# The next chunk's scores ahead of the gate or modulation unit in TensorE's order of a chunked recurrence

## The chip, the cores and the metric

The kernel runs on one core of a Trainium2 chip. A core has five engines that run their own instruction streams and meet only at semaphores: TensorE (PE, matrix products into PSUM; its weight loads are listed as PEld), VectorE (DVE), ScalarE (ACT), GpSimd (POOL) and SyncE (SP, which here only issues DMAs). The metric is the device time of one launch in microseconds (us).

## What is computed

One inference step of a hybrid decoder layer: two gated linear recurrences side by side (GLA with 4 heads, HGRN2 with 8 heads), gated norms, a merge, a layer norm, a mixture of 64 experts and a second layer norm, for 512 prompt tokens and 8 single decode tokens. The change lies in the prompt's recurrences. Cut to these:

```python
def _gated_linear_recurrence(q, k, v, log_a, s0):
    ...
    def step(s, inp):
        qi, ki, vi, gi = inp
        b = jnp.cumsum(gi, axis=2)
        diff = b[:, :, :, None, :] - b[:, :, None, :, :]
        decay = jnp.exp(jnp.where(mask, diff, -jnp.inf))
        scores = jnp.einsum('bhik,bhjk,bhijk->bhij', qi, ki, decay)
        o = jnp.einsum('bhij,bhjv->bhiv', scores, vi) + jnp.einsum('bhik,bhkv->bhiv', qi * jnp.exp(b), s)
        b_last = b[:, :, -1:, :]
        s_new = s * jnp.exp(b_last[:, :, 0, :, None]) + jnp.einsum('bhjk,bhjv->bhkv', ki * jnp.exp(b_last - b), vi)
        return s_new, o
    ...
```

Each output row is then normed by its root mean square (the root that POOL makes below) and multiplied by a gate of a projection: silu for GLA, sigmoid for HGRN2 (the gate units below).

## The kernel before

All data is float32. The prompt's recurrences are three **groups** of four heads each: group 0 is GLA (256 values per head), groups 1 and 2 are the two halves of HGRN2 (128 values per head). A group has 16 **chunks** of 128 tokens (4 heads x 4 chunks), numbered c = 0 to 15, and chunks go in **pairs** (2k, 2k+1), since the decay factors are made for 256 tokens at a time. Between the groups PE makes the projections of the next one.

Every engine's order is written out by hand, and no scheduler moves anything. An engine takes its instructions strictly in that order.

**PE**, in `recurrence_pe`, loops over c. `update(c)` (L530) is the product that gives the state's increment; it needs `kdT`, the copy that ACT makes (L652) of a transposed factor. `fill` is a piece of other work put into the loop: in group 0 half of a modulation projection (`mod_proj`, L839, 4 products of 512 columns, and in every second chunk `mod_turn`, L848, ahead of it), in groups 1 and 2 one gate projection (`gate_proj`, L865, 8 products of 260 columns). `scores_of(c+1)` makes the next chunk's transposed factor (L511), one block of scores (L513) and 14 blocks of 64x64 (L520); its first wait, on `s_Mq`, is for the pair's factors from DVE. `output(c)` (L537, L540) needs the summed scores of chunk c and ACT's `scale` of chunk c-1 (`s_on`), since both use one PSUM bank. `turn(c-1)` (L548) transposes the output before.

**DVE**, for every c: `mask` (L1631 to L1642, sums the seven levels of scores), `new_state` (L1655 or L1658), in groups 1 and 2 `gate_value` (L595 to L604), then for odd c `diffs` (L1607, eight differences of the pair after the next one) and for even c from 2 to 12 `factored` (L1622 to L1625), which turns the exponentials of pair c/2+1 into the factors that PE's `scores_of(c+2)` waits for. In group 2 DVE takes the turned output too (L1667).

**ACT**, for every c: `square(c-1)` (L659), `take_o` (L677, groups 0 and 1), `gate_tanh` (L588, groups 1 and 2), `scale(c-1)` (L664), then for even c from 2 to 12 `decays(c/2+1)`: Abs (L625) and Exp (L627) over 2048 columns, and after these `copy_kd(c+1)` (L652, L654). In group 0 `copy_rows` (L1230) stands at the head of every second chunk's list. Abs waits for `diffs` of its pair, and stands behind `scale` in ACT's order. **POOL** makes the root of the mean square between `square` and `scale` (L1427, L1429), and applies a gate in group 1 (L612).

The first two pairs' factors of a group are made before its loop (`first_factors`, and DVE's two first `factored`). So six pairs in each group, 2 to 7, have theirs made inside the loop.

Of the kernel before, what the change touches and what calls it, by code (L numbers as in the profile page):

```python
# [128 lines left out]
def decoder_step(nc, xT, small, wgk2, const, route, wq, wexp, st_in, yT, st_prompt, st_out):  # L129
    with ExitStack() as ctx:  # L130
# [306 lines left out]
        def taken(gi, what):  # L437

            return 1 + max(n for n, it in enumerate(ITEMS) if it[:2] == (gi, what))

        def since(eng, s, value):

            if value > 0:
                eng.wait_ge(s, value)
# [33 lines left out]
        FILL = [[("mod", 8 + c) for c in range(16)], [("gate", c) for c in range(16)], [("gate", 16 + c) for c in range(16)]]  # L478
# [23 lines left out]
        def recurrence_pe(pe, gi, fill, last):  # L502
            v, base = GROUPS[gi]["v"], 16 * gi

            def scores_of(n):
                pair, p, c, h, cc = n // 2, n // 2 % 2, n % 2, n // 4 % 4, n % 4
                col_ = slice(c * CH, (c + 1) * CH)
                pe.wait_ge(s_Mq, pair + 1)
                since(pe, s_kdc, n)
                since(pe, s_L0, n)  # L510
                pe.transpose(ps[:, 2, 0:CH], M[:, p, 7, col_], ident)  # L511
                first, second = (slice(c * CH + h2 * HC, c * CH + (h2 + 1) * HC) for h2 in range(2))
                pe.matmul(ps[0:HC, 2, CH:CH + HC], M[:, p, 0, first], M[:, p, 0, second],  # L513
                          start=True, stop=True, tile_position=(0, 0)).then_inc(s_kdt, 1)
                since(pe, s_pm, 3 * n - 5)
                for l in range(1, LEV + 1):
                    for h2, part in enumerate((first, second)):
                        at = slice(cc * CH + h2 * HC, cc * CH + (h2 + 1) * HC)
                        lhs, rhs = (M[:, p, l, part], M[:, p, l, part]) if l < LEV else (k4[:, h, at], q4[:, h, at])
                        mm = pe.matmul(ps[h2 * HC:(h2 + 1) * HC, n % 2, (l - 1) * HC:l * HC], lhs, rhs,  # L520
                                       start=True, stop=True, tile_position=(0, h2 * HC))
                mm.then_inc(s_sc, 1)

            def values(n):
                return V[:, n % 4, n // 4 % 4 * v:(n // 4 % 4 + 1) * v]

            def update(n):
                pe.wait_ge(s_kdc, n + 1)
                since(pe, s_state, n)
                pe.matmul(ps[:, 3, 0:v], kdT[:, n % 2, :], values(n), start=True, stop=True).then_inc(s_u, 1)  # L530

            def output(n):
                o = ps[:, 4, 0:v]
                pe.wait_ge(s_st, n + 1)
                pe.wait_ge(s_L0, n + 1)
                since(pe, s_on, n)
                mm = pe.matmul(o, ST[:, n % 2, :], values(n), start=True, stop=(n % 4 == 0))  # L537
                if n % 4:
                    pe.wait_ge(s_state, n)
                    mm = pe.matmul(o, M[:, n // 2 % 2, 8, n % 2 * CH:(n % 2 + 1) * CH], state[:, n % 4 % 2, 0:v],  # L540
                                   start=False, stop=True)
                mm.then_inc(s_o, 1)

            def turn(n):
                pe.wait_ge(s_on, n + 1)
                since(pe, s_oc, n)
                for j in range(v // P):
                    mm = pe.transpose(ps[:, 6, j * P:(j + 1) * P], on[n % 2][:, j * P:(j + 1) * P], ident)  # L548
                mm.then_inc(s_ot, 1)

            pe.wait_ge(s_zev, taken(gi, "v"))
            pe.wait_ge(s_sz, 1)
            scores_of(base)
            for c in range(17):
                if c < 16:
                    update(base + c)
                    fill(*FILL[gi][c])
                if c + 1 < 16:
                    scores_of(base + c + 1)
                if c < 16:  # L560
                    output(base + c)
                if c:
                    turn(base + c - 1)
            if gi == 0:
                last()
# [259 lines left out]
        def _(pe):  # L825
# [54 lines left out]
            for gi, what, a, b in ITEMS:  # L880
                g = GROUPS[gi]
                if gi and n == taken(gi - 1, "v"):
                    recurrence_pe(pe, gi - 1, fill, lambda: mod_turn(11))
                    pe.wait_ge(s_pm, 48 * gi)
                    pe.wait_ge(s_L0, 16 * gi)
# [32 lines left out]
                mm.then_inc(s_z, 1)  # L918
                n += 1
            recurrence_pe(pe, 2, fill, None)  # L920

            pe.wait_ge(s_zev, len(ITEMS))
# [1257 lines left out]
```

## Time and profile before

| | |
|---|---|
| runs | 1832.88, 1833.12, 1836.98 us; median 1833.12 |
| profiled execution | 1830.96 us, its span 1828.9 us |
| PE busy | 1690.9 us, 92% of the span |
| DVE, ACT, POOL busy | 32%, 25%, 16% of the span |
| granted clock of PE, mean over the span | 0.971 |
| group 0 / 1 / 2 | about 172 to 264 / 356 to 456 / 543.6 to 642.4 us |

Times in the rows are microseconds from the span's start. A row of the timeline is one instruction or a run of equal ones: its start, its length, engine, line, operation, what is written and read, the count, and in brackets the idle time of the engine just before it with what ended that. A long product is listed as two records. Matmuls overlap, so the time that a step takes is read from the start of its first row to the start of the next step's first row. The granted clock is the share of full speed that the chip gave PE: 1.00 is 2.4 GHz, 0.50 is 1.2 GHz.

### The profile page before, as it was taken

The page shows a single profiled execution, that of the slowest core. Times are in us where ns is not written, and L with a number is a line of the kernel's source. Part 1 is how long each engine was busy: PE and PEld are TensorE (multiplying, and loading weights), DVE is VectorE, ACT ScalarE, POOL GpSimd, SP SyncE. Part 2 cuts the span into 40 slices and gives each one's busy share as a digit, 9 for nine tenths or more (in the row PEclk, how much of TensorE's full clock was granted, in tenths as well). Part 3 has the DMA queues.
Part 4 walks back from the last instruction along what each step waited for, and adds up shares of the span by engine and source line. Part 5 has one row for each costly group of instructions (what it writes and reads, how often), then busy time and mean ns, then how long its engine had stood idle before and what let it go on. Part 6 is the DMA issues. An engine that isn't in the chain of part 4 may idle for free.

```text
span 1828.9 us, 26402 instructions
## 1 busy us (share of the span) xinstructions
PE 1690.9 (92%) x8996; PEld 1121.6 (61%) x8996; DVE 579.2 (32%) x1494; ACT 458.1 (25%) x1040; POOL 298.9 (16%) x488
## 2 busy tenths in 40 slices
PE   5999789998999999889998789999999999999985
PEld 2854558577858788678887544554444454444474
DVE  1213750587048733200125811111111111111145
ACT  1314651455134433200002111111111111111223
POOL 0000110023001110000000622222222222222410
PEclk8999999999999999989999789999999999999997
DMA  9213441210120099463111379999999999999361
GB/s 399 81 47 124 170 180 47 93 49 22 76 83 12 4 370 349 155 279 138 57 69 48 138 308 408 418 406 398 403 404 406 402 395 394 382 384 383 148 299 47
DMA packets 57197, 410.31 MB, mean 224 GB/s; under 512 B 12955, under 2 KB 18716, under 8 KB 29986
## 3 DMA queue, kind: packets, MB, share of 16 engines
q1 hardware_dynamic: 36210, 365.65, 50.4%
q0 software_dynamic: 19184, 42.58, 6.1%
q10 hardware_dynamic: 1728, 1.05, 0.2%
q8 instruction: 51, 0.84, 0.2%
q14 instruction: 24, 0.20, 0.0%
HBM read 391.79 MB, written 42.07 MB: 237 GB/s over the span
## 4 chain that ended last, share of the span: by engine, by line
PE 69%; DMA 12%; DVE 9%; ACT 5%; issue 2%; POOL 2%; SPq 0%; POOLq 0%; ACTq 0%; DVEq 0%
PE ps L957 12%; PE ps L1116 11%; PE ps L916 9%; DMA arena<-wexp 9%; PE ps L894 6%; PE ps L1121 5%; PE ps L1140 5%; PE ps L1147 3%; PE ps L997 3%; PE ps L865 2%; DVE arena L1622 2%; ACT arena L625 2%; PE ps L1187 2%; ACT arena L627 2%; PE ps L1102 2%
## 5 line engine op out<-in xcount | busy, mean ns | idle before, releaser
L1116 PE MATMUL ps<-arena 128*128 128x512 f32 x592 | 263.0, 597 | 10.6 <-DMA arena<-wexp 8.9
L1116 PEld LDWEIGHTS ps<-arena 128*128 128x128 f32 x592 | 110.3, 191 | 149.9 <-issue 149.9
L916 PE MATMUL ps<-Hb,arena 128*128 128x260 f32 x768 | 174.0, 391 | 0.0
L916 PEld LDWEIGHTS ps<-Hb,arena 128*128 128x128 f32 x768 | 149.4, 195 | 24.2 <-ACT arena L1260 0.7
L2066 DVE TENSOR_TENSOR arena<-ps,arena 128x256 f32<-128x256 f32 x73 | 26.2, 359 | 413.6 <-ACT arena L1374 413.6
L1485 POOL DMA_INDIRECT yrows<-arena x72 | 74.6, 1036 | 427.4 <-issue 427.4
L957 PE MATMUL ps<-Hb,arena 128*128 128x260 f32 x512 | 125.1, 400 | 14.9 <-DMA arena<-wq 14.4
L1121 PE MATMUL ps<-arena 128*64 128x256 f32 x1152 | 132.3, 382 | 1.7 <-DMA arena<-wexp 0.8
L1140 PE MATMUL ps<-arena 128*128 128x512 f32 x288 | 129.6, 593 | 0.0
L2075 DVE COPY arena<-ps 128x512 f32<-128x512 f32 x108 | 74.6, 691 | 154.5 <-PE ps L1140 108.2
L957 PEld LDWEIGHTS ps<-Hb,arena 128*128 128x128 f32 x512 | 101.6, 200 | 33.1 <-DMA arena<-wq 15.0
L1374 ACT ACTIVATE arena<-ps 128x256 f32<-128x256 f32 x73 | 24.2, 331 | 374.8 <-PE ps L1116 257.6
L865 PE MATMUL ps<-Hb,arena 128*128 128x260 f32 x512 | 117.5, 383 | 0.0
L894 PE MATMUL ps<-arena,Hb 128*128 128x512 f32 x256 | 112.0, 596 | 0.0
L1121 PEld LDWEIGHTS ps<-arena 128*64 128x64 f32 x1152 | 82.6, 137 | 41.5 <-issue 8.0
L865 PEld LDWEIGHTS ps<-Hb,arena 128*128 128x128 f32 x512 | 94.9, 190 | 13.0
L1622 DVE TENSOR_TENSOR arena<-arena 128x256 f32<-128x256 f32 x168 | 60.1, 427 | 101.0 <-ACT arena L627 101.0
L894 PEld LDWEIGHTS ps<-arena,Hb 128*128 128x128 f32 x256 | 48.0, 190 | 64.1 <-issue 60.7
L1140 PEld LDWEIGHTS ps<-arena 128*128 128x128 f32 x288 | 52.0, 190 | 51.6 <-issue 51.6
L1367 ACT ACTIVATE arena<-ps 128x512 f32<-128x512 f32 x111 | 62.4, 595 | 38.7 <-PE ps L1102 37.1
L1758 DVE TENSOR_TENSOR arena<-arena,ps 128x260 f32<-128x260 f32 x32 | 13.6, 424 | 180.7 <-PE ps L957 180.6
L1476 POOL DMA_INDIRECT Hb<-h2rows,arena x58 | 62.5, 1078 | 49.6 <-POOL arena L1474 47.0
(339 smaller groups left out, 2231.8 us busy)
## 6 DMA issues: line engine op xcount, KB each, us to landing
arena<-wexp SPq DMA_DIRECT2D x73, 2048.0 KB, 16.5
arena<-wq SPq DMA_DIRECT2D x44, 2048.0 KB, 7.9
arena<-wexp SPq DMA_DIRECT2D x72, 1024.0 KB, 19.3
arena<-yrows SPq DMA_DIRECT2D x4, 4096.0 KB, 22.5
arena<-st_in SPq DMA_DIRECT2D x8, 1024.0 KB, 10.0
Xb<-vs POOLq DMA_DIRECT2D x16, 512.0 KB, 9.6
st_out<-arena SPq DMA_DIRECT2D x8, 1024.0 KB, 9.9
Xb<-xT SPq DMA_DIRECT2D x2, 2080.0 KB, 17.6
```

Of the source, the lines that this page charges most:

```text
L865: mm = pe.matmul(ps[:, bank, 0:HALF], ring[:, q % 4, m % 4, c, :], H[:, c, lo:lo + HALF], start=(c == 0), stop=(c == KC - 1))
L894: mm = pe.matmul(ps[:, bank, :], H[:, c, b * P:(b + 1) * P], ring[:, q % 4, :, c, :], start=(c == 0), stop=(c == KC - 1))
L916: mm = pe.matmul(ps[:, bank, 0:HALF], ring[:, q % 4, a, c, :], H[:, c, halves[b][0]:halves[b][1]], start=(c == 0), stop=(c == KC - 1))
L957: mm = pe.matmul(ps[:, 5 + k % 3, 0:HALF], ring[:, (Q_P + n) % 4, u, c, :], (H, oa, H, ob)[u][:, c, lo:hi], start=(c == 0), stop=(c == KC ...
L1116: mm = pe.matmul(ps[:, 0, :], xe[:, 0, c, :], GU[k % 4][:, c, :], start=(c == 0), stop=(c == KC - 1))
L1121: mm = pe.matmul(ps[h * SS:(h + 1) * SS, 1, 0:FE], x, GUs[k % 4][:, c, h, :, :], start=(c == 0), stop=(c == KC - 1), tile_position=(0, h * ...
L1140: mm = pe.matmul(ps[:, 4 + hf, :], aT[:, 0, f, :], WD[k % 4][:, f, hf * 512:(hf + 1) * 512], start=(f == 0), stop=(f == 1))
L1367: act.activation(xe[:, k % 2, 4 * hf:4 * hf + 4, :].rearrange("p c n -> p (c n)"), ps[:, 6 + hf, :], ACT.Copy).then_inc(s_xc, 1)
L1476: pool.indirect_dma_start(out=xg[k % 4][:, 0:n], out_offset=None, in_=rows, in_offset=bass.IndirectOffsetOnAxis(ap=idg[:, k % 4:k % 4 + 1] ...
L1485: pool.indirect_dma_start(out=rows, out_offset=bass.IndirectOffsetOnAxis(ap=ida[:, k:k + 1], axis=0), in_=yb[:, k % 2, 0:n], in_offset=Non ...
L1622: dve.tensor_tensor(e, e, kq, ALU.mult)
L2075: dve.tensor_copy(yb[:, k % 2, hf * 512:(hf + 1) * 512], ps[:, 3 if k % 2 else 4 + hf, :]).then_inc(s_yc, 1)
```

## The change

In PE's loop over the chunks the call of `fill` moves from ahead of `scores_of(c+1)` to behind it. Each chunk's list was update, fill, scores of the next chunk, output, turn, and is update, scores of the next chunk, fill, output, turn. Nothing is added or removed, every instruction keeps its waits, and the other four engines' lists are unchanged.

```diff
             for c in range(17):
                 if c < 16:
                     update(base + c)
-                    fill(*FILL[gi][c])
                 if c + 1 < 16:
                     scores_of(base + c + 1)
                 if c < 16:
+                    fill(*FILL[gi][c])
                     output(base + c)
                 if c:
                     turn(base + c - 1)
```

Group 0, PE, a chunk with odd c, before. L530 is the update, L839 the modulation half, L511 to L520 the scores of the next chunk, whose first product waits for the pair's factors (`mq_mk_done`), L537 the output:

```order
L530 MATMUL ps<-arena,Xb 128x256 [waits state_done,kd_copied]
L839 MATMUL ps<-arena,OB 32x512 [waits quad_loaded_3]
L839 MATMUL ps<-arena,OB 32x512 x3
L511 MATMUL ps<-cst,arena 128x128 [waits halves_copied,kd_copied,mq_mk_done]
L513 MATMUL ps<-arena 64x64
L520 MATMUL ps<-arena 64x64 [waits score_sums]
L520 MATMUL ps<-arena 64x64 x13
L537 MATMUL ps<-arena,Xb 128x256 [waits o_scaled,halves_copied,scores_summed]
```

The same chunk now:

```order
L530 MATMUL ps<-arena,Xb 128x256 [waits state_done,kd_copied]
L511 MATMUL ps<-cst,arena 128x128 [waits halves_copied,kd_copied,mq_mk_done]
L513 MATMUL ps<-arena 64x64
L520 MATMUL ps<-arena 64x64 [waits score_sums]
L520 MATMUL ps<-arena 64x64 x13
L839 MATMUL ps<-arena,OB 32x512 [waits quad_loaded_3]
L839 MATMUL ps<-arena,OB 32x512 x3
L537 MATMUL ps<-arena,Xb 128x256 [waits o_scaled,halves_copied,scores_summed]
```

The modulation half stood between the update and the wait for the factors; it now stands between that wait and the output.

Groups 1 and 2, PE, a chunk before, with L865 the gate projection:

```order
L530 MATMUL ps<-arena,Xb 128x128 [waits state_done,kd_copied]
L865 MATMUL ps<-Hb,arena 128x260 [waits gate_value,quad_loaded_3]
L865 MATMUL ps<-Hb,arena 128x260 x7
L511 MATMUL ps<-cst,arena 128x128 [waits halves_copied,kd_copied,mq_mk_done]
L513 MATMUL ps<-arena 64x64
L520 MATMUL ps<-arena 64x64 [waits score_sums]
L520 MATMUL ps<-arena 64x64 x13
L537 MATMUL ps<-arena,Xb 128x128 [waits o_scaled,halves_copied,scores_summed]
```

The same chunk now:

```order
L530 MATMUL ps<-arena,Xb 128x128 [waits state_done,kd_copied]
L511 MATMUL ps<-cst,arena 128x128 [waits halves_copied,kd_copied,mq_mk_done]
L513 MATMUL ps<-arena 64x64
L520 MATMUL ps<-arena 64x64 [waits score_sums]
L520 MATMUL ps<-arena 64x64 x13
L865 MATMUL ps<-Hb,arena 128x260 [waits gate_value,quad_loaded_3]
L865 MATMUL ps<-Hb,arena 128x260 x7
L537 MATMUL ps<-arena,Xb 128x128 [waits o_scaled,halves_copied,scores_summed]
```

Eight products of 260 columns have moved from ahead of the scores to the place just ahead of the output.

## Rows read from the trace of the kernel before

**Rows 1.** PE's waits by who ended them: us in total, times, longest.

```profile
PE ps L530 <- ACT Xb L652: 18.4, 16, 1.5
```

**Rows 2.** PE's timeline, group 0, chunk 9 (a row of chunk 5 at half clock ahead).

```profile
201.31 0.47 PE L511 MATMUL ps<-cst,arena 128*128 128x128 f32 x1 [0.59 <-DVE arena L1625]
...
203.62 1.22 PE L537 MATMUL ps<-arena,Xb 128*128 128x256 f32 x2
...
223.70 0.70 PE L530 MATMUL ps<-arena,Xb 128*128 128x256 f32 x2 [1.49 <-ACT Xb L652]
224.33 1.07 PE L839 MATMUL ps<-arena,OB 128*32 128x512 f32 x8
226.74 0.33 PE L511 MATMUL ps<-cst,arena 128*128 128x128 f32 x1 [1.34 <-DVE arena L1625]
...
228.48 0.70 PE L537 MATMUL ps<-arena,Xb 128*128 128x256 f32 x2 [0.34 <-DVE Xb L1642]
```

**Rows 3.** DVE's timeline, group 0, from one pair's factors to the next pair's.

```profile
223.51 2.50 DVE L1622 TENSOR_TENSOR arena<-arena 128x256 f32<-128x256 f32 x7 [1.82 <-ACT arena L627]
...
226.26 0.42 DVE L1625 TENSOR_TENSOR arena<-arena 128x256 f32<-128x256 f32 x1
...
235.63 2.50 DVE L1622 TENSOR_TENSOR arena<-arena 128x256 f32<-128x256 f32 x7 [1.76 <-ACT arena L627]
```

**Rows 4.** ACT's timeline, group 0: square, scale and Abs after output 9.

```profile
229.64 0.38 ACT L659 ACTIVATE Xb<-ps 128x256 f32<-128x256 f32 x1 [1.24 <-PE ps L540]
...
231.38 0.47 ACT L664 ACTIVATE Xb<-ps,tiny 128x256 f32<-128x256 f32 x1 [0.75 <-POOL tiny L1429]
231.75 1.90 ACT L625 ACTIVATE arena<-arena 128x2048 f32<-128x2048 f32 x1
```

**Rows 5.** PE's timeline, group 1, chunk 5: update, gate projection, scores, output.

```profile
387.17 0.49 PE L530 MATMUL ps<-arena,Xb 128*128 128x128 f32 x2 [1.40 <-ACT Xb L652]
387.49 3.67 PE L865 MATMUL ps<-Hb,arena 128*128 128x260 f32 x16
391.00 0.27 PE L511 MATMUL ps<-cst,arena 128*128 128x128 f32 x1
...
392.28 0.49 PE L537 MATMUL ps<-arena,Xb 128*128 128x128 f32 x2
```

**Rows 6.** DVE's timeline, group 1, from one pair's factors to the next pair's.

```profile
386.98 2.51 DVE L1622 TENSOR_TENSOR arena<-arena 128x256 f32<-128x256 f32 x7 [1.40 <-ACT arena L627]
...
389.74 0.42 DVE L1625 TENSOR_TENSOR arena<-arena 128x256 f32<-128x256 f32 x1
...
399.76 2.51 DVE L1622 TENSOR_TENSOR arena<-arena 128x256 f32<-128x256 f32 x7 [1.47 <-ACT arena L627]
```

**Rows 7.** ACT's timeline, group 1: square, scale and Abs after output 5.

```profile
393.03 0.28 ACT L659 ACTIVATE Xb<-ps 128x128 f32<-128x128 f32 x1 [1.08 <-PE ps L540]
...
394.60 0.37 ACT L664 ACTIVATE Xb<-ps,tiny 128x128 f32<-128x128 f32 x1 [0.67 <-POOL tiny L1429]
395.88 1.91 ACT L625 ACTIVATE arena<-arena 128x2048 f32<-128x2048 f32 x1 [0.91 <-DVE arena L1607]
```

**Rows 8.** PE's timeline, group 2: the outputs of chunks 3 and 13.

```profile
566.99 0.49 PE L537 MATMUL ps<-arena,Xb 128*128 128x128 f32 x2
...
629.19 0.49 PE L537 MATMUL ps<-arena,Xb 128*128 128x128 f32 x2
```

**Rows 9.** Windows, PE alone: window, its length, busy (instructions), granted clock, DMA share, GB/s.

```profile
196.80:199.00 2.20, 0.73 (x6) 1.00 0.03 7
199.20:205.60 6.40, 5.81 (x44) 0.50 0.60 202
222.20:226.70 4.50, 1.70 (x11) 1.00 0.19 36
639.90:642.70 2.80, 0.65 (x3) 1.00 0.08 23
642.90:646.10 3.20, 3.20 (x8) 0.50 0.85 253
```

## The prediction

> **What bounds the kernel now.** The change touches the three recurrences alone, some 290 of the 1828.9 us, so I read those and take the rest as unmoved. First PE's waits: the largest inside the loop is the update's for `kdT`, 18.4 us over 16 times [rows 1]. It invites the thought that PE sets the pace and waits for small copies. Then the timelines of PE, DVE and ACT over one pair of chunks, to see what the pair's period is made of. In group 0 DVE starts one pair's factors at 223.51 and the next pair's at 235.63, 12.12 us apart [rows 3], and both starts wait for ACT's Exp (L627). In group 1 the same distance is 12.78 us, 386.98 to 399.76 [rows 6]. PE waits in every such pair: 1.49 and 1.34 us in group 0 [rows 2], 1.40 us in group 1 [rows 5]. So PE follows. What leads is a **ring of DVE and ACT**: factors of a pair, masks, state, gate value, differences of the next pair, Abs, Exp, factors again. That ring has no PE step in it: in group 1 Abs starts after 0.91 us of idle that the differences end [rows 7], so ACT was free before. In group 0 Abs follows `scale` at once [rows 4], so there the two conditions for Abs, differences done and scale done, fall almost together. Group 2 has five periods in 629.19 - 566.99 = 62.20 us, 12.44 each [rows 8].
>
> **The change, part by part.** No instruction comes or goes, no queue but PE's changes, and no wait is new. What moves is the fill: 1.07 us in group 0 [rows 2], 391.00 - 387.49 = 3.51 us in groups 1 and 2 [rows 5].
>
> *Even chunks c.* The next scores belong to the same pair and find their factors ready. PE does the same five steps in another order, between the same two outputs. The update, scores and output start when they did or earlier, and nobody who waits for them is on the ring. I cost this at nothing; its cover is that PE waits later in the pair anyway. Bounds: a gain of at most the update waits, 18.4 us [rows 1], taken up as a rival below; no loss, since no step's inputs come later. The first chunks of groups 1 and 2 and the last two of each group are bound by PE's own work and only change order: zero too.
>
> *Odd chunks c, six in each group (c = 3 to 13).* Here the next scores belong to the next pair, and their first product waits for DVE's factors. Before, the fill ran inside that wait: in group 0 it takes 1.07 of the 226.74 - 224.33 = 2.41 us between update and scores [rows 2], and in group 1 the factors are ready at 389.74 + 0.42 + 0.06 = 390.22 (0.06 is the hop from the last factor, 226.26 + 0.42, to PE's start at 226.74 [rows 2, 3]), while the fill runs until 391.00 [rows 5, 6]. Now PE stands idle until the factors come, does the scores, **and only then the fill, with the output behind it**. The output is what ACT's square waits for, scale follows square, and Abs of the next pair stands behind scale in ACT's list. So a second ring appears, through PE: factors, scores, fill, output, square, root, scale, Abs, Exp, factors.
>
> Its length in group 0: factors to PE's start 226.74 - 223.51 = 3.23; scores 392.28 - 391.00 = 1.28; fill 1.07; output's start to square 229.64 - 228.48 = 1.16; square to Abs 231.75 - 229.64 = 2.11; Abs to the next factors 235.63 - 231.75 = 3.88 [rows 2 to 5]. Sum 12.73 against 12.12, so 0.61 a pair. The mask is no obstacle: it let output 9 start 228.48 - 226.74 = 1.74 after the factors, and scores and fill take 2.35. Six pairs: the first output is late by 2.35 - 1.74 = 0.61 too, and five rings follow. **6 x 0.61 = 3.7 us.**
>
> In group 1: 390.22 - 386.98 = 3.24; scores 1.28; fill 3.51; output to square 393.03 - 392.28 = 0.75; square to scale 394.60 - 393.03 = 1.57; scale to Abs 231.75 - 231.38 = 0.37; Abs to the next factors 399.76 - 395.88 = 3.88 [rows 4 to 7]. Sum 14.60 against 12.78: 1.82 a pair. The first output after such a wait comes at 390.22 + 4.79 = 395.01 instead of 392.28, 2.7 late (the same phase in chunk 3 as here in chunk 5). **2.7 + 5 x 1.82 = 11.8 us.** The differences, bound before, now end in time: the old ring is shorter by those 1.82.
>
> Group 2 has the same steps on PE and ACT; I take the 14.60 there. **2.7 + 5 x (14.60 - 12.44) = 13.5 us.** Together 3.7 + 11.8 + 13.5 = **29.0 us**. The least certain term is square to scale, which could be some 0.2 shorter once POOL and DVE are quiet beside it: 10 x 0.2 = 2 us less.
>
> *The clock.* PE's idle time bunches up. In groups 1 and 2 one idle of 390.22 - 387.17 - 0.49 = 2.56 us follows each odd update, with some 1 us more ahead of it; in group 0 an idle of 2.41 follows one of 1.49, with only the update between [rows 2, 5]. Before, PE worked 1.70 of 4.50 us in that place, and the clock stayed at 2.4 GHz in this pair; but two pairs earlier it was at 1.2 GHz for all of 199.20 to 205.60, after a stretch with 0.73 us of work in 2.20. After the last output of group 2, 0.65 in 2.80, it fell again, for at least 3.20 us [rows 9]. The new stretches hold less work than any of these: about 0.6 us in 4.5 in group 0, 0.5 in 3.5 in groups 1 and 2. I expect the clock to fall in most pairs, and to be low just while scores, fill and output run, which are now on the ring. At 1.2 GHz the scores take 203.62 - 201.31 = 2.31 us instead of 1.28 [rows 2, 5]. In group 0 scores, fill and output all at half clock would cost 1.03 + 1.07 + about 0.6 = 2.7; the fall may come a little late, so 2.1. In groups 1 and 2 the 4.79 us of scores and fill are longer than half a low spell: spells of 3.20 to 6.40 us [rows 9] lose half their length, 1.6 to 3.2; I take 2.5. With a fall in four of six pairs, of which group 0 had one already: 3 x 2.1 + 8 x 2.5 = **26.3 us**. Bounds: none, and every pair at the upper costs, 5 x 2.7 + 12 x 3.2 = 52.
>
> The Trainium skill, "TensorE: Matmul & The Clock Gate", section on HAM oscillation, says that a loop whose matmuls are parted by a long wait starts every turn on a cold clock, and that shorter idle gaps are safe. None of my idle stretches alone is as long as the gap named there, so by that page the clock would stay high and the sum be 29. The rows speak against it: the clock fell where PE had been idle for 2.20 - 0.73 = 1.47 us [rows 9].
>
> Sum: 29.0 + 26.3 = 55.3 us. The profiled execution took 1830.96, so it would take 1886.3; the median of the runs lies 2.2 above it, so **1888.4**.
>
> **The rivals.** (a) *The clock stays high.* The ring through PE is all: 1833.1 + 29.0 = 1862. For it: most pairs of group 0 kept 2.4 GHz with 1.70 us of work in 4.50. Against: rows 9's two falls. (b) *Faster: PE sets the pace after all.* The scores of each chunk, and with them the transposed factor, come a fill earlier, ACT copies it earlier, and the update's wait goes: at most 18.4 us [rows 1], 1833.1 - 18.4 = 1815. It decides if the copy waits for PE and not for ACT's own list. Against: the update waits in odd chunks, where Exp stands right ahead of the copy, and Exp waits for DVE's ring. (c) *No difference.* The output waits for something else as long, so that the fill is hidden in its new place too: the mask would have to let the output go 4.8 us after the factors and not 1.74 [rows 2]. Then 1833. (d) *Slower than forecast*: a fall in every pair, 29 + 52 = 81 at the most, 1914.
>
> **How the numbers follow.** Forecast (clock falls in many pairs, 1874 to 1906) 0.62; (a) 1855 to 1874, 0.25; (b) 0.03; (c) 0.05; (d) above 1906, 0.05. From 1855 to 1906 that is 0.87, and I allow some of it for a ring that I sized wrongly: the range is 1855 to 1906. A measurement tells about 0.3%, 5.5 us, from no change. Faster 0.03, same 0.05, slower 0.92.
>
> **What would show it.** In the trace after: PE's wait of some 2.5 us ahead of L511 in each odd chunk, ended by L1625, six in each group; in groups 1 and 2 L865 directly ahead of L537; Abs (L625) no longer waiting for L1607 but following L664; pair periods of 12.7 us in group 0 and 14.6 in groups 1 and 2 where the clock is 1.00, and 15 to 18 where it is 0.50. The three groups should be longer by about 10, 22 and 23 us, and nothing after them. I am wrong if the periods stay at 12.1, 12.8 and 12.4, or if Abs starts before the odd output's scale.

## The result

| | median of the runs | lowest to highest | ratio to before |
|---|---|---|---|
| before, on the same chip | 1834.55 us (4 runs) | 1832.88 to 1836.98 | |
| after | 1881.82 us (4 runs) | 1874.53 to 1888.27 | 1.0255, 95% interval 1.0215 to 1.0295 |

The changed kernel is slower by 47.3 us, 2.55%. The prediction said 1888.4 us, 1855 to 1906, slower. The profiled execution was the slowest of the four: 1888.27 us, against 1830.96 before, so the traces show 57.3 us where the medians show 47.3. The runs spread over 13.7 us, against 4.1 before, and the slower a run, the lower its mean granted clock: 0.951, 0.956, 0.957 and 0.961 for 1888.27, 1881.98, 1881.66 and 1874.53 us. That fits a clock that falls in more or in fewer pairs of chunks, which only the profiled execution can show pair by pair.

The page's line on the engines, after. The other engines do the same work in the same time as before (DVE and ACT were 32% and 25%); PE's busy time rises by 32.3 us from 1690.9 without one instruction more, because some matmuls run at half the clock:

```profile
PE 1723.2 (91%) x8996; PEld 1144.2 (61%) x8996; DVE 580.3 (31%) x1494; ACT 456.7 (24%) x1040; POOL 295.3 (16%) x488
```

PE's waits after. The update's wait, the one of [rows 1], shrinks from 18.4 to 6.8 us. Whoever follows that wait alone would call it a gain. The wait ahead of the scores grows by more. It came six times before, and is now there in all eighteen odd chunks in question. The first line is of before, the other two are of after:

```profile
PE ps L511 <- DVE arena L1625: 7.3, 6, 1.3
PE ps L511 <- DVE arena L1625: 44.6, 18, 2.6
PE ps L530 <- ACT Xb L652: 6.8, 8, 1.4
```

PE in group 1, after, answering to [rows 5]. The gate projection (L865) stands directly ahead of the output (L537). The two outputs are 409.30 - 393.31 = 15.99 us apart; the clock fell in the second of these chunks, which its L865 shows (5.37 against 3.77 us):

```profile
388.37 0.33 PE L511 MATMUL ps<-cst,arena 128*128 128x128 f32 x1 [2.55 <-DVE arena L1625]
...
389.70 3.77 PE L865 MATMUL ps<-Hb,arena 128*128 128x260 f32 x16
393.31 0.38 PE L537 MATMUL ps<-arena,Xb 128*128 128x128 f32 x2
...
399.68 0.49 PE L530 MATMUL ps<-arena,Xb 128*128 128x128 f32 x2 [0.21 <-ACT Xb L652]
402.72 0.33 PE L511 MATMUL ps<-cst,arena 128*128 128x128 f32 x1 [2.55 <-DVE arena L1625]
...
404.09 5.37 PE L865 MATMUL ps<-Hb,arena 128*128 128x260 f32 x16
409.30 0.38 PE L537 MATMUL ps<-arena,Xb 128*128 128x128 f32 x2
```

DVE in the same place, answering to [rows 6], from one pair's factors to the next, 399.50 - 385.14 = 14.36 us at full clock. Between them stand the next differences (L1607), which end at 390.68 + 3.31 = 393.99:

```profile
385.14 2.50 DVE L1622 TENSOR_TENSOR arena<-arena 128x256 f32<-128x256 f32 x7 [4.09 <-ACT arena L627]
...
390.68 3.31 DVE L1607 TENSOR_TENSOR arena<-arena 128x256 f32<-128x256 f32 x8
...
399.50 2.50 DVE L1622 TENSOR_TENSOR arena<-arena 128x256 f32<-128x256 f32 x7 [2.99 <-ACT arena L627]
```

ACT beside it, answering to [rows 7]. Square (L659) waits 4.59 us for the output. Abs (L625) follows `scale` (L664) without an idle, where it had waited 0.91 us for the differences; these have been ready for 1.6 us when it starts. In the whole trace Abs waited for the differences 7.3 us over ten times before, and after it never waits:

```profile
393.95 0.28 ACT L659 ACTIVATE Xb<-ps 128x128 f32<-128x128 f32 x1 [4.59 <-PE ps L540]
...
395.35 0.37 ACT L664 ACTIVATE Xb<-ps,tiny 128x128 f32<-128x128 f32 x1 [0.50 <-POOL tiny L1429]
395.62 1.90 ACT L625 ACTIVATE arena<-arena 128x2048 f32<-128x2048 f32 x1
397.55 1.91 ACT L627 ACTIVATE arena<-arena 128x2048 f32<-128x2048 f32 x1
```

The lengths used from here on are distances between rows of L537 in the profiled executions. A group's length is that from its first output to its last; a period is the distance of two outputs of odd chunks.

| group | before | after | longer by | predicted |
|---|---|---|---|---|
| 0 | 85.09 us | 96.46 us | 11.4 | about 10 |
| 1 | 90.95 us | 110.10 us | 19.2 | 22 |
| 2 | 89.08 us | 112.52 us | 23.4 | 23 |

Together 54.0 of the profiled 57.3 us, so the loss lies in the three recurrences. The other 3.3 us lie behind the last output of group 2 (1192.9 us to the end of the span, against 1189.7 before), and nothing here explains them.

### The profile page after: what moved, and what is told of

Read it like the earlier page. It is cut to its first block, busy times and chain, and to the rows that moved or that the text cites. A ratio compares the mean times of both kernels' runs of the same rounds, so it can differ in the third digit from the quotient of the medians.

```text
span 1886.2 us, 26402 instructions
## 1 busy us (share of the span) xinstructions
PE 1723.2 (91%) x8996; PEld 1144.2 (61%) x8996; DVE 580.3 (31%) x1494; ACT 456.7 (24%) x1040; POOL 295.3 (16%) x488
## 4 chain that ended last, share of the span: by engine, by line
PE 72%; DMA 12%; DVE 6%; ACT 6%; issue 2%; POOL 2%; SPq 0%; POOLq 0%; ACTq 0%; DVEq 0%
PE ps L957 11%; PE ps L1116 10%; PE ps L916 9%; DMA arena<-wexp 9%; PE ps L894 6%; PE ps L1121 5%; PE ps L1140 5%; PE ps L865 5%; PE ps L1147 3%; PE ps L997 3%; DVE arena L1622 2%; ACT arena L627 2%; PE ps L1187 2%; ACT arena L625 2%; PE ps L520 2%
## 5 line engine op out<-in xcount | busy, mean ns | idle before, releaser
L916 PE MATMUL ps<-Hb,arena 128*128 128x260 f32 x768 | 171.9, 387 | 0.0
L916 PEld LDWEIGHTS ps<-Hb,arena 128*128 128x128 f32 x768 | 147.7, 193 | 23.9 <-ACT arena L1260 0.7
L957 PE MATMUL ps<-Hb,arena 128*128 128x260 f32 x512 | 124.1, 398 | 14.5 <-DMA arena<-wq 14.0
L865 PE MATMUL ps<-Hb,arena 128*128 128x260 f32 x512 | 135.4, 423 | 0.0
L957 PEld LDWEIGHTS ps<-Hb,arena 128*128 128x128 f32 x512 | 100.9, 198 | 32.5 <-DMA arena<-wq 14.7
L865 PEld LDWEIGHTS ps<-Hb,arena 128*128 128x128 f32 x512 | 105.2, 211 | 19.8
L1147 PE MATMUL ps<-arena 128*64 128x512 f32 x288 | 69.7, 605 | 0.0
```

Source lines behind the costliest of these rows:

```text
L865: mm = pe.matmul(ps[:, bank, 0:HALF], ring[:, q % 4, m % 4, c, :], H[:, c, lo:lo + HALF], start=(c == 0), stop=(c == KC - 1))
L916: mm = pe.matmul(ps[:, bank, 0:HALF], ring[:, q % 4, a, c, :], H[:, c, halves[b][0]:halves[b][1]], start=(c == 0), stop=(c == KC - 1))
L957: mm = pe.matmul(ps[:, 5 + k % 3, 0:HALF], ring[:, (Q_P + n) % 4, u, c, :], (H, oa, H, ob)[u][:, c, lo:hi], start=(c == 0), stop=(c == KC ...
L1147: mm = pe.matmul(ps[h * SS:(h + 1) * SS, 3, :], aT[:, 1, 0, f * SS:(f + 1) * SS], WD[k % 4][:, f, h * 512:(h + 1) * 512], start=(f == 0), ...
```

## The experiments

The theory: a ring of factors, scores, fill, output, square, scale, Abs, Exp, factors sets the pace (the loss in length), and the clock falls in the gap ahead of the scores (the rest). The rivals: the even chunks have a part in it; the clock has none; or the loss is in what PE itself waits for.

Each run was timed beside runs of its own of the kernel before, with medians of 1832.86 (`e1` to `e4`), 1833.52 (`e5` to `e8`) and 1833.92 us (`e9`, `e10`), against 1834.55 in the result. Where two kernels are compared below, the difference is that of their distances to their own before. The ratios behind the times are to that before, with the 95% interval.

**One half of the change at a time.** `e1_even` has the new order in even chunks alone:

```diff
                 if c < 16:
                     update(base + c)
+                    if c % 2:
+                        fill(*FILL[gi][c])
                 if c + 1 < 16:
                     scores_of(base + c + 1)
                 if c < 16:
-                    fill(*FILL[gi][c])
+                    if c % 2 == 0:
+                        fill(*FILL[gi][c])
                     output(base + c)
```

> The fill goes behind the next scores in even chunks only; odd chunks keep the old order. My theory (only the odd chunks, whose next scores wait for DVE's factors, put the fill on the ring): no difference from before, 1834 us within 3, pair periods 12.1, 12.8 and 12.4 us. Rival (the later fills and gates cost something in every chunk): about half of the 47 us, so some 1858.

Measured: 1831.12 us against 1832.86, ratio 0.9992 (0.9981 to 1.0003). Group lengths 85.09, 90.76 and 88.98 us, within 0.2 us of those of before. The even chunks cost and bring nothing that the runs could tell.

`e2_odd` is the reverse, with the two conditions exchanged.

> The fill goes behind the next scores in odd chunks only. My theory: the whole loss is here, 1875 to 1888 us like the changed kernel, periods of 14.3 us at 2.4 GHz and 16 to 17 with the clock low. Rival (every chunk costs): about 1858.

Measured: 1898.23 us, ratio 1.0354 (1.0337 to 1.0371). The odd chunks alone lose 18.1 us more than the whole change (16.4 between the bare medians, the 16 us of the expectation of `e8_odd_filler`). Where they come from is seen in groups 1 and 2, which are 118.34 and 118.30 us long and not 110.10 and 112.52, 14 us together. The windows of PE in group 1 of `e2_odd` (window, its length, busy time and count, granted clock, DMA share, GB/s), laid where the clock changes:

```profile
398.60:404.90 6.30, 4.31 (x46) 1.00 0.00 0
405.10:411.70 6.60, 6.11 (x40) 0.50 0.04 12
411.90:421.90 10.00, 8.29 (x69) 1.00 0.00 0
422.10:428.70 6.60, 5.96 (x40) 0.50 0.00 0
```

The twelve periods of groups 1 and 2 are all 17.07 to 17.44 us long, and each has such a spell of half clock of 6.8 us, which covers scores and fill. In the changed kernel the same spell stands in six of these periods, one of 3.4 us in two, and four stayed at full clock. The windows in group 1, a short spell, a long one, and what PE did in the gap before the long one:

```profile
404.10:407.30 3.20, 3.20 (x9) 0.50 0.07 20
...
445.00:448.20 3.20, 1.38 (x10) 1.00 0.00 0
448.50:455.00 6.50, 6.07 (x40) 0.50 0.00 1
```

So `e2_odd` has the same ring with more falls. What makes them more is told with `e8_odd_filler` below.

**The clock alone.** `e3_filler` is the changed kernel with five products of a constant into the PSUM bank that the scores write next, in the gap. Their result is overwritten by the scores. The line with `since` is the scores' own wait for that bank, taken ahead of the products.

```diff
                 if c < 16:
                     update(base + c)
+                    if c % 2 and 3 <= c <= 13:
+                        since(pe, s_pm, 3 * (base + c + 1) - 5)
+                        for _ in range(5):
+                            pe.matmul(ps[:, (c + 1) % 2, 0:256], ident, C("reset")[:, 0:256], start=True, stop=True)
                 if c + 1 < 16:
                     scores_of(base + c + 1)
```

> The changed kernel, and in the 18 odd chunks where PE waits some 2.3 to 2.5 us for the factors, five products of 256 columns (about 0.43 us each) that write a score bank which the next scores overwrite: PE stays busy, nothing else waits for them. Theory of two parts (ring through PE, and clock): the clock stays at 1.00 and only the ring is left, 3.7 + (2.7 + 5 x 1.57) + (2.7 + 5 x 1.82) = 26 us over before, 1860 us. Ring alone: no change against the changed kernel, 1882. Clock alone: back to 1835.

Measured: 1860.74 us, ratio 1.0159 (1.0138 to 1.0181), 27.9 us over before, 19.4 less than the changed kernel. The windows of groups 1 and 2 of `e3_filler` (busy time of PE, its weight loads, DVE, ACT and POOL, each with its count, then the granted clock) have the clock at 1.00 throughout, where the changed kernel had 0.92 and 0.89:

```profile
356.00:470.00 114.00, 110.30 (x924) 91.12 (x923) 79.71 (x225) 51.70 (x135) 24.95 (x53) 1.00 0.11 40
565.00:680.00 115.00, 110.12 (x888) 93.45 (x887) 76.71 (x237) 46.17 (x118) 13.92 (x35) 1.00 0.09 33
```

PE's rows of `e3_filler` in one gap (its line numbers are four higher behind the edit). The filler takes 2.32 us of the 397.65 - 394.93 = 2.72 us, and the scores still wait 0.40 us for the factors, so it delays nobody (four of the twelve periods of the changed kernel kept the clock without a filler, and are 14.26 to 14.27 us long as well):

```profile
394.60 0.49 PE L530 MATMUL ps<-arena,Xb 128*128 128x128 f32 x2 [0.21 <-ACT Xb L656]
394.93 2.32 PE L560 MATMUL ps<-cst 128*128 128x256 f32 x10
397.65 0.33 PE L511 MATMUL ps<-cst,arena 128*128 128x128 f32 x1 [0.40 <-DVE arena L1629]
```

The twelve periods of groups 1 and 2 are 14.26 to 14.37 us: the ring without the clock, predicted at 14.60. Group lengths are 91.79, 101.36 and 100.89 us. In group 0 three periods are 12.43 to 12.59 (predicted 12.73) and three 14.31 to 14.35, where the clock still fell for some 3.4 us. So the ring is real without the clock, and the clock's part is real as well.

`e8_odd_filler` puts the same filler into `e2_odd`.

> e2_odd (fill behind the next scores in odd chunks only), which took 16 us more than the full change, with the five filler products of e3_filler. If the 16 us are the clock (it fell in all of the 18 pairs there), this takes the same 1860 us as e3_filler. If they are the order of the even chunks, it stays 16 us above, 1876.

Measured: 1863.73 us, ratio 1.0171 (1.0145 to 1.0196); groups 91.67, 101.66 and 101.01 us, within 0.3 us of `e3_filler` each. With the same filler, and so the clock at 1.00 in groups 1 and 2, the two orders are alike (27.9 and 30.2 us over before); the 18 us between `e2_odd` and the changed kernel are therefore the clock's, but for some 2 us. In the even chunk ahead of the gap the work just before the output is the gate projection in the changed kernel, and the scores' small blocks in `e2_odd`. That this is what makes the clock fall more often was not tested.

**The ring, cut in one link.** `e4_decays_first` is the changed kernel with ACT's Abs and Exp ahead of square and scale instead of behind them:

```diff
                 if gi == 0 and c % 2 == 0 and c:
                     copy_rows(3 + c // 2)
+                if c and gi:
+                    gate_tanh(act, filled(gi, c - 1))
+                if even:
+                    decays(act, 8 * gi + c // 2 + 1)
                 if c:
                     square(base + c - 1)
                 if c >= 2 and gi < 2:
                     take_o(base + c - 2)
-                if c and gi:
-                    gate_tanh(act, filled(gi, c - 1))
                 if c:
                     scale(base + c - 1)
-                if even:
-                    decays(act, 8 * gi + c // 2 + 1)
```

> The changed PE order, and ACT issues Abs and Exp ahead of square, take_o and scale (gate_tanh stands ahead of Abs). This cuts the link from scale to Abs, on which my ring through PE rests. My theory: the period falls back to the ring of DVE and ACT, 12.1, 12.8 and 12.4 us, 1835 to 1850 us, the upper end if the clock still falls. Rival (PE is late whatever ACT does, because the fill stands behind the factors): PE's idle of 2.5 us stays and so does the time, 1875 or more.

Measured: 1839.49 us, ratio 1.0039 (1.0026 to 1.0051), so 41 us below the changed kernel with PE's order untouched. Groups 87.04, 97.50 and 90.55 us. Group 1 keeps 6.5 us of loss: its periods alternate between 13.06 and 14.9, and the clock fell in two of them. ACT's rows, of one of these two, show the rest of the ring. Abs has left scale, but `gate_tanh` (L588) stands ahead of it and waits 5.74 us for the gate projection, the fill itself:

```profile
397.35 0.39 ACT L588 ACTIVATE side<-ps 128x260 f32<-128x260 f32 x1 [5.74 <-PE ps L865]
397.63 1.90 ACT L625 ACTIVATE arena<-arena 128x2048 f32<-128x2048 f32 x1
```

**The fill out of the ring.** `e5_fill_last` is the changed kernel with the fill behind the output, so that scores and output both come ahead of it:

```diff
                 if c < 16:
-                    fill(*FILL[gi][c])
                     output(base + c)
+                    fill(*FILL[gi][c])
```

> The changed kernel with the fill moved once more, behind the output. If only the place between scores and output mattered, the output would come early again and the time fall to 1835. By my ring the fill stays on the path through ACT: gate_tanh (groups 1 and 2) waits for the gate projection and stands ahead of scale, and copy_rows (group 0) waits for the modulation half and stands ahead of square. Ring in groups 1 and 2: 3.24 + 1.28 + 0.33 + 3.51 + 0.3 + 0.39 + 0.37 + 3.88 = 13.3 us, in group 0 about 12.9; without clock falls 1849, with them up to 1874.

Measured: 1876.99 us, ratio 1.0236 (1.0211 to 1.0262), above the 1849 to 1874 that were expected. The periods are 14.0 in group 1 and 13.9 in group 2 where the clock stayed high, and not the 13.3 that the expectation worked out. ACT's rows of `e5_fill_last` in group 1 show what I had missed. `take_o` (L677) waits 3.25 us for the turned output (L548), and scale and Abs stand behind `take_o` in ACT's list:

```profile
397.62 0.28 ACT L659 ACTIVATE Xb<-ps 128x128 f32<-128x128 f32 x1 [1.49 <-PE ps L540]
...
401.24 0.37 ACT L677 ACTIVATE OB<-ps,tiny 128x128 f32<-128x128 f32 x1 [3.25 <-PE ps L548]
401.51 0.38 ACT L588 ACTIVATE side<-ps 128x260 f32<-128x260 f32 x1
401.78 0.37 ACT L664 ACTIVATE Xb<-ps,tiny 128x128 f32<-128x128 f32 x1
402.03 1.92 ACT L625 ACTIVATE arena<-arena 128x2048 f32<-128x2048 f32 x1
```

PE's rows of the same place show why: that turn now comes behind the fill as well.

```profile
397.20 0.39 PE L540 MATMUL ps<-arena 128*128 128x128 f32 x2
397.42 3.67 PE L865 MATMUL ps<-Hb,arena 128*128 128x260 f32 x16
400.93 0.27 PE L548 MATMUL ps<-cst,arena 128*128 128x128 f32 x1
```

From the start of a pair's factors to the square it is now 397.62 - 391.91 = 5.71 us, and was 393.95 - 385.14 = 8.81. Of these 3.1 us only 0.4 arrive at Abs (402.03 - 391.91 = 10.12 against 395.62 - 385.14 = 10.48).

In group 0, which is 18.2 us longer than before, the link is the one that the expectation named. `copy_rows` stands ahead of the square and waits for the modulation half; the scores there ran at half clock, and the periods are 13.87 to 15.62 us:

```profile
211.81 0.60 ACT L1230 ACTIVATE side<-ps 128x512 f32<-128x512 f32 x1 [4.03 <-PE ps L839]
212.30 0.38 ACT L659 ACTIVATE Xb<-ps 128x256 f32<-128x256 f32 x1
```

A piece of work can be moved past one reader and still stand ahead of another.

**Both rings cut.** What the rings have in common is that Abs comes late in ACT's list and that DVE makes the differences late. `e6_early_diffs` is the changed kernel with Abs and Exp at the head of ACT's list and the differences directly behind the factors, one chunk earlier:

```diff
+                if even:
+                    decays(act, 8 * gi + c // 2 + 1)
                 if gi == 0 and c % 2 == 0 and c:
                     copy_rows(3 + c // 2)
...
                 if c:
                     scale(base + c - 1)
-                if even:
-                    decays(act, 8 * gi + c // 2 + 1)
...
-                    if c % 2 and c <= 11:
-                        diffs(8 * gi + (c + 3) // 2)
+                    if c == 1:
+                        diffs(8 * gi + 2)
...
                         factored(8 * gi + c // 2 + 1)
+                        if c <= 10:
+                            diffs(8 * gi + c // 2 + 2)
```

> The changed PE order; DVE makes the differences of the next pair directly behind a pair's factors (ahead of mask, new_state and gate value), and ACT issues Abs and Exp ahead of square and scale. Both rings are cut: what is left is differences, Abs, Exp, factors, 2.7 + 3.9 + 3.2 = 9.8 us, below PE's own work of 11.4 us a pair in groups 1 and 2 and below DVE's 10.5 in group 0. My theory: periods of 10.5 to 11.2, 11.4 and 11.4 us, faster than before by 5 x 1.3 + 5 x 1.4 + 5 x 1.0 = 18 us, 1815 us. Rival (the fill behind the scores costs by itself): above 1834.

Measured: 1818.88 us, ratio 0.9929 (0.9903 to 0.9955), so faster than both kernels: 14.6 us below before, 62 below the changed one. Groups 77.28, 88.00 and 86.32 us: group 0 gained 7.8 us where 6.5 were expected, groups 1 and 2 only 3.0 and 2.8 where 7 and 5 were. ACT's rows of `e6_early_diffs` in group 1: Abs waits 1.65 us for the differences, with scale 2.2 us done, and that scale is of the output before the odd one, so the ring through PE is cut.

```profile
391.91 0.37 ACT L664 ACTIVATE arena<-ps,tiny 128x128 f32<-128x128 f32 x1 [0.52 <-POOL tiny L1429]
...
394.52 1.91 ACT L625 ACTIVATE arena<-arena 128x2048 f32<-128x2048 f32 x1 [1.65 <-DVE arena L1607]
```

DVE's rows just before: it waits 1.23 us for `gate_tanh` (L588), which stands behind Exp, and from there to the next pair's factors at 399.54 it is never idle.

```profile
387.78 0.42 DVE L595 SCALAR_TENSOR_TENSOR side<-side,ps 128x260 f32<-128x260 f32 x1 [1.23 <-ACT side L588]
388.12 3.02 DVE L1622 TENSOR_TENSOR arena<-arena 128x256 f32<-128x256 f32 x7
```

`e9_tanh_between` goes after that wait: `e6_early_diffs` with `gate_tanh` between Abs and Exp.

```diff
-        def decays(act, pair):
+        def decays(act, pair, between=None):
...
+            if between is not None:
+                gate_tanh(act, between)
...
-                    decays(act, 8 * gi + c // 2 + 1)
+                    decays(act, 8 * gi + c // 2 + 1, filled(gi, c - 1) if gi else None)
...
-                if c and gi:
+                if c and gi and not even:
                     gate_tanh(act, filled(gi, c - 1))
```

> e6_early_diffs, with gate_tanh of even ACT turns issued between Abs and Exp and not behind Exp. In e6_early_diffs DVE's gate value waited up to 3.9 us for that tanh (9.4 us in group 1), which made every second pair 12.6 us and not 11.4. Theory: periods of 11.4 to 11.5 us throughout groups 1 and 2, 5 us less than e6_early_diffs, 1813 us. Rival (something else holds those pairs): no gain over e6_early_diffs.

Measured: 1816.18 us, ratio 0.9902 (0.9885 to 0.9919). Periods of 11.3 to 11.8 us in groups 1 and 2 (the first of group 1 is 12.22), which are 84.51 and 85.37 us long: 3.5 and 1.0 less than in `e6_early_diffs`. Group 0, where the two kernels are the same, came out 1.7 us longer, so two profiles of the same work can differ by that much. The intervals of the two overlap, so in the time the step is likely, not settled. It is the fastest version of this study, 17.7 us below before.

**Is the new order of PE good once the rings are gone?** `e7_early_diffs_old_order` has the edits of `e6_early_diffs` on the kernel before, and so PE's old order.

> The same edits on DVE and ACT as in e6_early_diffs, with the old PE order (fill ahead of the scores). My theory: PE's own work is the bound in groups 1 and 2, so its order is worth nothing: 1815 us, within 4 us of e6_early_diffs. Rival (the change's order is better or worse in itself): a difference of over 10 us.

Measured: 1829.43 us, ratio 0.9979 (0.9966 to 0.9992), 10.5 us slower than `e6_early_diffs`, where at most 4 were expected. Groups 87.89, 88.44 and 86.53 us: the difference is in group 0 alone, 87.89 against 77.28. PE's rows of `e7_early_diffs_old_order` there. The turn of the modulation (L848) waits 1.97 us for ACT's `copy_rows` (L1230), which stands behind Exp now, and the scores are queued behind it:

```profile
212.51 1.06 PE L848 MATMUL ps<-cst,side 128*128 128x9 f32 x8 [1.97 <-ACT side L1230]
213.50 1.06 PE L839 MATMUL ps<-arena,OB 128*32 128x512 f32 x8
214.49 0.33 PE L511 MATMUL ps<-cst,arena 128*128 128x128 f32 x1
```

These waits come to 26.8 us over twelve times in `e7_early_diffs_old_order`, and to 12.1 over eight in `e6_early_diffs`, where the scores have already gone (L511 at 194.99):

```profile
194.99 0.27 PE L511 MATMUL ps<-cst,arena 128*128 128x128 f32 x1
...
197.28 1.06 PE L848 MATMUL ps<-cst,side 128*128 128x9 f32 x8 [0.95 <-ACT side L1230]
```

`e10_old_order_rows_first` tests that: `e7_early_diffs_old_order` with `copy_rows` ahead of Abs.

```diff
-                if even:
-                    decays(act, 8 * gi + c // 2 + 1)
                 if gi == 0 and c % 2 == 0 and c:
                     copy_rows(3 + c // 2)
+                if even:
+                    decays(act, 8 * gi + c // 2 + 1)
                 if c:
                     square(base + c - 1)
```

> e7_early_diffs_old_order (old PE order), with copy_rows of group 0 back ahead of Abs and Exp. In e7_early_diffs_old_order PE's mod_turn waited for copy_rows behind Exp, with the next scores queued behind it: group 0 took 88 us against 77 with the new order. Theory (that queue is the whole difference between the orders): group 0 falls by some 8 us, 1820 us. Rival (the fill ahead of the scores costs in another way in group 0): no change, 1829.

Measured: 1824.57 us, ratio 0.9952 (0.9939 to 0.9965), 5.3 us less than `e7_early_diffs_old_order`, with group 0 at 83.00 us, 4.9 less. PE's rows of L848 there have no wait for L1230 any more. That is half of the 10.6 us. Of the other half the trace shows a part. The output waits for ACT in group 0 (the rows are PE's, of `e10_old_order_rows_first`), and group 0 had 13.7 us of half clock in this profile (spells of 3.4 and 10.2 us), 6.8 more than in that of `e6_early_diffs`:

```profile
221.28 0.33 PE L511 MATMUL ps<-cst,arena 128*128 128x128 f32 x1
...
223.86 0.67 PE L537 MATMUL ps<-arena,Xb 128*128 128x256 f32 x2 [1.17 <-ACT Xb L664]
```

Half clock loses at most half its length, so the clock can stand for at most 3.4 of the 5.7 us between the two group lengths. The rest was not separated further. The new order with `copy_rows` first, which would be the fair partner of `e10_old_order_rows_first`, was not run.

| kernel | us | over its before | group 0 | group 1 | group 2 |
|---|---|---|---|---|---|
| after | 1881.82 | +47.3 | 96.46 | 110.10 | 112.52 |
| e1_even | 1831.12 | -1.7 | 85.09 | 90.76 | 88.98 |
| e2_odd | 1898.23 | +65.4 | 96.67 | 118.34 | 118.30 |
| e3_filler | 1860.74 | +27.9 | 91.79 | 101.36 | 100.89 |
| e8_odd_filler | 1863.73 | +30.2 | 91.67 | 101.66 | 101.01 |
| e4_decays_first | 1839.49 | +6.6 | 87.04 | 97.50 | 90.55 |
| e5_fill_last | 1876.99 | +43.5 | 103.24 | 104.90 | 103.46 |
| e6_early_diffs | 1818.88 | -14.6 | 77.28 | 88.00 | 86.32 |
| e7_early_diffs_old_order | 1829.43 | -4.1 | 87.89 | 88.44 | 86.53 |
| e9_tanh_between | 1816.18 | -17.7 | 78.95 | 84.51 | 85.37 |
| e10_old_order_rows_first | 1824.57 | -9.4 | 83.00 | 90.01 | 86.48 |

## Why the prediction was right

**What bounds the kernel.** Shown. With PE's list untouched and only ACT's changed, the loss fell from 47.3 to 6.6 us (`e4_decays_first`); with the old order of PE and only ACT and DVE changed, the kernel became faster (`e7_early_diffs_old_order`, `e10_old_order_rows_first`). Both say that the ring, and not PE, sets the pace. Rival (b), a gain from the update's wait, is out: the wait did fall, by 11.6 us, and nothing came of it.

**Even chunks at nothing.** Shown by `e1_even`, 0.9992.

**The ring through PE.** Its links, measured in the rows of group 1 above and in the answers of the same view between them: factors to scores 388.37 - 385.14 = 3.23 (predicted 3.24), scores 1.33 (1.28), fill 3.61 (3.51), output to square 0.64 (0.75), square to scale 1.40 (1.57), scale to Abs 0.27 (0.37), Abs to factors 3.88 (3.88). Sum 14.36 against 14.60. The link that is off most, by 0.17 us, is square to scale, the one that the prediction called uncertain, and in the way it said; that it is because POOL and DVE are quiet beside it was not tested. Three others are off by 0.10 to 0.11. In group 0 the ring is 12.43 to 12.59, not 12.73.

The price of the ring without the clock is an estimate from `e3_filler`. Group 1 is 101.36 - 90.95 = 10.4 us longer (predicted 11.8), group 2 100.89 - 89.08 = 11.8 (13.5). Group 0 is 6.7 us longer, of which three falls take 3 x 1.9 = 5.7, while before had one of its own, which made two of its periods 0.6 us longer; that leaves some 2.2 (3.7). Together about **24 us where 29.0 was predicted**. That is the term that was too large.

**The clock.** The ring's 24 leave 47.3 - 24 = 23 us in the medians and 54.0 - 24.4 = 30 in the profiled execution, against 26.3 predicted. So the forecast of 1888.4 was 6.6 us above the median, ring and clock both too high. That the profiled execution took 1888.27 is luck: there the ring was 4.6 us less than predicted and the clock some 4 us more. The two factors of the clock's term were both somewhat off. It fell in 14 of 18 pairs of the profiled execution (six, four, four by group), and in 12 by the forecast. A fall cost 1.7 us when the spell was short (15.99 and 16.05 against 14.27) and 2.8 to 3.0 when it was long (17.1 to 17.3 against 14.27), where I had 2.5; in group 0 1.4 to 1.9, where I had 2.1.

One step of the working for groups 1 and 2 did not come true. It put about 1 us of idle ahead of the update, beside the 2.56 ahead of the scores. The update waited 0.21 us in two of the twelve pairs and not at all in the others, and PE was busy for 0.95 us of the 3.50 ahead of the scores at 448.93 us, where the clock fell and the prediction had 0.5. The clock fell all the same.

The windows of the three groups, after, answering to [rows 9]; over the same work before, the clock was 0.96 in group 0 and 1.00 in groups 1 and 2:

```profile
172.00:275.00 103.00, 81.78 (x797) 50.59 (x795) 71.51 (x206) 55.12 (x137) 14.01 (x31) 0.88 0.46 168
356.00:480.00 124.00, 107.46 (x857) 86.23 (x856) 81.48 (x229) 54.90 (x135) 23.18 (x50) 0.92 0.10 37
565.00:700.00 135.00, 116.49 (x887) 94.31 (x886) 85.65 (x262) 52.94 (x130) 14.53 (x36) 0.89 0.07 25
```

Rival (a), the clock that stays high, had 0.25. The longest single idle in these loops is 2.55 us ahead of the scores, and the clock fell at it in most pairs. The Trainium skill, "TensorE: Matmul & The Clock Gate", section on HAM oscillation, warns of idle gaps longer than that; that shorter ones are safe is what the prediction drew from it. The trace does not bear that out. The 1862 us that the rival gave is close to what `e3_filler` measured, 1860.7, though with a smaller ring and three falls left in group 0. Rivals (c) and (d) are out: no period stayed, and the falls were not in every pair.

**What would show it.** The wait of 2.5 us ahead of L511, six in each group; L865 directly ahead of L537; Abs behind L664: all as written. The periods at full clock in groups 1 and 2 were 14.27 for 14.6. With the clock low they were 15.99 to 17.3 us there, within the 15 to 18, but 13.85 to 14.35 in group 0, below it. The ring of 12.7 in group 0 can't be seen in the changed kernel itself, since the clock fell in all six pairs there; `e3_filler` shows 12.4.

**What the prediction did not see** is that the order of PE is not bad in itself. It loses because ACT's list ties Abs to the output. With that tie cut, the same change is worth 10.5 us (`e6_early_diffs` against `e7_early_diffs_old_order`); about half of that is the wait of the modulation's turn, which the edits to ACT's list had brought, and which the new order lets the scores past. Against the old order with that wait taken away (`e10_old_order_rows_first`) it is ahead by 5.3 us, but the 95% intervals of the two overlap (0.9903 to 0.9955 and 0.9939 to 0.9965), so that rest is likely and not settled.

## What to carry to other kernels

Follow the chain around one full period, through every engine, before you move work on one of them: here an engine with 92% busy time was not the one that set the pace, and a move that shortened its largest wait in the loop put work of its own onto the ring, 3.6 us a pair in groups 1 and 2. Where a loop's engines wait for one another in strict order, ask of each instruction which unrelated one stands ahead of it; taking Abs out from behind `scale` and making the differences a chunk earlier gave back 62 us in the changed kernel, more than the 47 that PE's order had cost. And price idle time on TensorE twice, once as time and once as the clock that it may cost to the matmuls behind it.

## What the runs showed of the hardware

- The granted clock fell to 0.50 at gaps whose longest idle was 2.55 us, and stayed low for 3.4 or 6.8 us. It did not fall at every such gap: of the twelve pairs of groups 1 and 2 in the changed kernel, all with the same 2.55 us, four kept 1.00 and eight did not.
- Five products of 256 columns in such a gap, which nobody reads, held the clock at 1.00 through 12 of 12 pairs of groups 1 and 2. They were worth 19.4 us in the changed kernel and 35.2 us in `e2_odd`, each over its own before. In group 0 they did so in three pairs of six.
- Where the half-clock spell covers scores and fill, one such period can follow another: in `e2_odd` they are 17.07 to 17.44 us, and the clock fell in six of six in each of groups 1 and 2. Why that pattern holds itself up is open.
